# Two matrix products cut into quarter parts and spread between the steps of the RWKV-7 head loop

## The reference

```python
r, w, k, v, kk, a = ...              # 16 heads of 64, from the input projection
def frame_step(S, inp):              # RWKV-7, 256 steps
    sa = jnp.einsum('bhvk,bhk->bhv', S, -kk_t)
    S = S * w_t + sa[..., None] * (kk_t * a_t) + v_t[..., None] * k_t
    return S, jnp.einsum('bhvk,bhk->bhv', S, r_t)
o = group_norm(o) * ln_g + ln_b + bonus      # per head
o = o * g                                    # gate
y_rwkv = o @ w_rwkv_proj
y_conv = silu(layernorm(conv(...))) @ w_conv_proj
merged = gate0 * y_rwkv + gate1 * y_conv
x = x + merged @ w_out
```

## Time and profile before

| what | value |
|---|---|
| median of 3 runs | 1508.72 us |
| the profiled execution | 1513.77 us, of which the span 1512.0 us |
| PE busy | 1340.9 us (89%), 7904 matmuls |
| DVE, ACT, POOL busy | 856.9, 716.8, 606.2 us |
| mean granted PE clock | 0.942 |

### The profile page before, as it was taken

How to read it: one execution, slowest core, us unless ns; L and a number is a source line. 1 busy time by engine, 2 the same in 40 slices (tenths; PEclk the granted TensorE clock), 3 DMA queues, 4 the chain that set the end, 5 groups by cost and what they waited for, 6 DMA issues and landing times. The chain is left out here.

```text
span 1512.0 us, 22529 instructions
## 1 busy us (share of the span) xinstructions
PE 1340.9 (89%) x7904; PEld 1076.1 (71%) x7904; DVE 856.9 (57%) x1454; ACT 716.8 (47%) x1225; POOL 606.2 (40%) x324
## 2 busy tenths in 40 slices
PE   5989988788899999998759998867899988799996
PEld 4877877576677777776547775756788866678885
DVE  2292354434688888887341799995777753210112
ACT  4455455434477666766444333444333423344442
POOL 5859668540000000001357654734100006578784
PEclk9999998689899999999979998888999999899999
DMA  6637443037399999997356444542000005356562
GB/s 201 177 109 200 137 139 125 1 103 236 116 342 302 320 318 316 325 299 229 96 164 188 130 128 139 168 119 95 18 2 2 2 23 175 114 154 189 170 189 84
DMA packets 127271, 239.88 MB, mean 159 GB/s; under 512 B 16297, under 2 KB 32347, under 8 KB 127185
## 3 DMA queue, kind: packets, MB, share of 16 engines
q1 hardware_dynamic: 116384, 227.12, 48.0%
q10 hardware_dynamic: 10801, 11.60, 2.8%
HBM read 234.49 MB, written 1.05 MB: 156 GB/s over the span
## 5 line engine op out<-in xcount | busy, mean ns | idle before, releaser
L292 POOL TENSOR_TENSOR wlo<-raw,whi 128x1024 fp32r<-128x1024 f32 (+1 forms) x232 | 564.6, 2452 | 712.4 <-ACT whi L287 711.9
L298 PE MATMUL bank<-whi,t0h 128*128 128x512 f32 (+1 forms) x1072 | 440.2, 411 | 22.1 <-POOL wlo L292 6.2
L287 ACT ACTIVATE whi<-raw 128x1024 fp32r<-128x1024 f32 (+1 forms) x300 | 309.0, 1052 | 275.1 <-PE bank L300 231.2
L299 PE MATMUL bank<-wlo,t0h 128*128 128x512 f32 (+1 forms) x1072 | 429.0, 400 | 0.0
L300 PE MATMUL bank<-whi,t0l 128*128 128x512 f32 (+1 forms) x1072 | 428.8, 400 | 0.0
L298 PEld LDWEIGHTS bank<-whi,t0h 128*128 128x128 f32 x1072 | 206.7, 193 | 78.5 <-issue 23.7
L300 PEld LDWEIGHTS bank<-whi,t0l 128*128 128x128 f32 x1072 | 206.3, 192 | 48.6
L299 PEld LDWEIGHTS bank<-wlo,t0h 128*128 128x128 f32 x1072 | 206.5, 193 | 45.8 <-issue 1.7
L292 DVE TENSOR_TENSOR wlo<-work,whi 128x1024 fp32r<-128x1024 f32 x96 | 113.0, 1218 | 7.5 <-ACT whi L287 7.4
L287 ACT ACTIVATE whi<-work 128x1024 fp32r<-128x1024 f32 x96 | 97.9, 1055 | 5.1 <-PE bank L1460 5.1
L292 DVE TENSOR_TENSOR wlo<-raw,whi 128x1024 fp32r<-128x1024 f32 x68 | 80.2, 1219 | 13.8 <-ACT whi L287 13.8
(11 more groups left out here) (421 smaller groups left out, 1889.7 us busy)
## 6 DMA issues: line engine op xcount, KB each, us to landing
raw<-in_w_ff SPq DMA_DIRECT2D x64, 512.0 KB, 3.7
raw<-in_w_in SPq DMA_DIRECT2D x60, 496.0 KB, 3.6
raw<-in_w_in SPq DMA_DIRECT2D x56, 512.0 KB, 3.7
work<-in_w_exp_down SPq DMA_DIRECT2D x68, 256.0 KB, 6.2
work<-in_w_exp_gate SPq DMA_DIRECT2D x62, 256.0 KB, 5.9
work<-in_w_exp_up SPq DMA_DIRECT2D x62, 256.0 KB, 7.0
raw<-in_w_exp_down SPq DMA_DIRECT2D x60, 256.0 KB, 5.4
raw<-in_w_exp_gate SPq DMA_DIRECT2D x34, 256.0 KB, 6.0
```

Of the source, the lines that this page charges most:

```text
L287: nc.scalar.activation(whi[:, s, 0:width], raw_of(n)[:, 0:width], ACT.Copy).then_inc(hi_ready, 1)
L292: ins = (nc.vector if split_by_vector(n) else nc.gpsimd).tensor_tensor(wlo[:, s, 0:width], raw_of(n)[:, 0:width], whi[:, s, 0:width].bitca ...
L298: nc.tensor.matmul(dst, hi, wh, start=first, stop=False)
L299: nc.tensor.matmul(dst, hi, wl, start=False, stop=False)
```

## The change

The last two quarters of Q_CONV (6 and 7) leave `first()` and are multiplied in step 0, in eight parts of six matmuls' third each (`quarter_part`: one position tile and one row block, three matmuls), at the places where later steps have the tail. The second half of Q_CONV goes to banks 6 and 7, and its gating moves behind mask 4 of step 0. The grams of pair 0 come one quarter earlier, and their second pair uses banks 3 and 2 as in the other steps.

Q_RWKV is taken in another order (`RWKV_TILES`): quarters 0 to 3 are now both column halves of input rows 0 to 511, so all four need only the first four turned chunks. The first two are cut into parts and stand in pair 7's tail. Its splits move: quarters 2 and 3 are split on ACT inside step 0 (behind levels 3 and 5), and quarters 4 and 5 in pair 7's tail. The three rows move to slots 1 to 3, so that slot 0 takes quarter 4 early; DVE's wait for them moves behind step 0. The diff, cut to what bears on this:

```diff
@@ -313,6 +313,17 @@
...
+def quarter_part(pe, n, q, dst, hi, lo, part):
...
+    if part == 0:
+        wait_low(pe, n)
+    wh, wl = pair_view(whi, n, TW), pair_view(wlo, n, TW)
+    t, kk = part // 2, part % 2
+    k, r = 2 * q + kk, slice(t * P, (t + 1) * P)
+    mm = times(dst[t][:, 0:TW], hi[:, k, r], lo[:, k, r], wh[:, kk, :], wl[:, kk, :], k == 0, k == KC - 1)
+    if part == 3:
+        mm.then_inc(quarter_done, 1)
@@ -1811,13 +1822,26 @@
...
-    load_square(sp, Q_RWKV, A["w_rwkv_proj_2"][0], range(4))
-    for j, (dst, name) in enumerate(((ka_row, "k_a_2"), (lng, "ln_x_g_2"), (lnb, "ln_x_b_2"))):
+    w = A["w_rwkv_proj_2"][0].rearrange("(k p) n -> p k n", k=KC)
...
+    def rwkv(j):
+        q, c = RWKV_TILES[j]
+        load(sp, Q_RWKV + j, [(pair_view(raw, Q_RWKV + j, TW), w[:, 2 * q:2 * q + 2, c * TW:(c + 1) * TW])])
...
+    for j in range(4):
+        rwkv(j)
+    for j, dst, name in ((1, ka_row, "k_a_2"), (2, lng, "ln_x_g_2"), (3, lnb, "ln_x_b_2")):
...
+    rwkv(4)
+    sp.wait_ge(*tok_ready.at(2 * PAIRS))
+    rwkv(5)
...
-    load_square(sp, Q_RWKV, A["w_rwkv_proj_2"][0], range(4, 8))
+    rwkv(6)
+    rwkv(7)
...
+RWKV_TILES = ((0, 0), (0, 1), (1, 0), (1, 1), (2, 0), (3, 0), (2, 1), (3, 1))
@@ -2176,9 +2200,9 @@
...
-ka_row, lng, lnb = (raw[:, (Q_RWKV + j) % RING, :] for j in range(3))
+ka_row, lng, lnb = (raw[:, (Q_RWKV + j) % RING, :] for j in range(1, 4))
...
-ka_first = carve(10880, P)
+ka_first = carve(10880, 2 * P)
@@ -2207,7 +2231,7 @@
...
-    return bank[(3 if u > 1 and not (isinstance(p, int) and p == 0) else 5) - u % 2]
+    return bank[(3 if u > 1 else 5) - u % 2]
@@ -2253,7 +2277,7 @@
...
-            pe.wait_ge(*gram_masked.at(4 * p + 2))
+            pe.wait_ge(*evac2.at(NT * len(TILES2)))
@@ -2355,28 +2379,47 @@
...
         if tail:
+            if p == 1:
+                pe.wait_ge(*conv_gated.at(4))
             rest(p - 1, c, 0)
+        else:
+            pe.wait_ge(*conv_gated.at(2))
+            conv_part(6, 0)
         if prep:
...
             solve(p - 1, c, 0)
+        else:
+            conv_part(6, 1)
         below(p, b, 0, (1,))
...
             state(p - 1, c)
+        else:
+            conv_part(6, 2)
         below(p, b, 1)
...
             outputs(p - 1, c, 0, 0)
+        else:
+            conv_part(6, 3)
         grow(p, b, 1)
...
             outputs(p - 1, c, 0, 1)
+        else:
+            conv_part(7, 0)
         below(p, b, 2)
...
             rest(p - 1, c, 1)
+        else:
+            conv_part(7, 1)
         grow(p, b, 2)
...
             solve(p - 1, c, 1)
+        else:
+            conv_part(7, 2)
         below(p, b, 3)
+        if not tail:
+            conv_part(7, 3)
         if tail:
@@ -2399,18 +2442,32 @@
...
+    def conv_quarter(n):
+        if n < 4:
+            pe.wait_ge(*c_low.at(n + 1))
+        wide_quarter(pe, Q_CONV + n, n % 4, bank[0:2] if n < 4 else bank[6:8], t0h, t0l)
...
+    def conv_part(n, part):
+        quarter_part(pe, Q_CONV + n, n % 4, bank[6:8], t0h, t0l, part)
...
+    def rwkv_part(j, part):
+        q, c = RWKV_TILES[j]
+        quarter_part(pe, Q_RWKV + j, q, bank[2 * c:2 * c + 2], t0h, t0l, part)
...
-        prepare = {0: lambda: decays(0), 2: lambda: turn_ar(0), 3: lambda: turn_bk(0, 0),
-                   5: lambda: grams(0, 0, (0, 1)), 6: lambda: grams(0, 0, (2, 3))}
-        for n in range(8):
-            if n < 4:
-                pe.wait_ge(*c_low.at(n + 1))
-            wide_quarter(pe, Q_CONV + n, n % 4, bank[2 * (n // 4):2 * (n // 4) + 2], t0h, t0l)
-            if n in prepare:
-                prepare[n]()
-        pe.wait_ge(*conv_gated.at(4))
+        conv_quarter(0)
+        decays(0)
+        conv_quarter(1)
+        conv_quarter(2)
+        turn_ar(0)
+        conv_quarter(3)
+        turn_bk(0, 0)
+        conv_quarter(4)
+        grams(0, 0, (0, 1))
+        conv_quarter(5)
+        grams(0, 0, (2, 3))
@@ -2433,20 +2490,28 @@
...
+        pe.wait_ge(*y_masked.at(2 * LEV * PAIRS))
+        pe.wait_ge(xt_copied, XT_COPIES * PAIRS)
+        pe.wait_ge(*turn_h.done(2))
+        rwkv_part(0, 0)
...
+        rwkv_part(0, 1)
+        rwkv_part(0, 2)
...
+        rwkv_part(0, 3)
+        rwkv_part(1, 0)
...
-        pe.wait_ge(*y_masked.at(2 * LEV * PAIRS))
-        pe.wait_ge(xt_copied, XT_COPIES * PAIRS)
-        for n in range(8):
-            if n < 4:
-                if n == 2:
-                    turn_h.pe(pe, [heads_gated.at(4), pair_done.at(PAIRS), (uo_copied, 2 * PAIRS)], (2, 3))
-                pe.wait_ge(*turn_h.done(2 * n + 2))
-            wide_quarter(pe, Q_RWKV + n, n % 4, bank[2 * (n // 4):2 * (n // 4) + 2], t0h, t0l)
+        for part in range(1, 4):
+            rwkv_part(1, part)
+        for j in range(2, 8):
+            if j == 4:
+                turn_h.pe(pe, [heads_gated.at(4), pair_done.at(PAIRS), (uo_copied, 2 * PAIRS)], (2, 3))
+            if j in (4, 5):
+                pe.wait_ge(*turn_h.done(2 * j - 2))
+            for part in range(4):
+                rwkv_part(j, part)
@@ -2518,12 +2583,16 @@
...
             head_roots(0)
+        if not tail:
+            split_high(act, Q_RWKV + 2)
         if prep:
...
         grown(p, b, 5)
+        if not tail:
+            split_high(act, Q_RWKV + 3)
         diagonal(p, b)
@@ -2537,7 +2606,7 @@
...
-        for q in range(4):
+        for q in range(2):
@@ -2555,7 +2624,9 @@
...
         copy_u(p, 1)
+        split_high(act, Q_RWKV + 4)
         head_roots(1)
+        split_high(act, Q_RWKV + 5)
@@ -2701,6 +2772,8 @@
...
+        else:
+            gate_convolution(1)
@@ -2741,7 +2814,7 @@
...
-            nc.vector.tensor_tensor(o, o, bank[2 * c + t][:, :], ALU.mult).then_inc(conv_gated.sem, 1)
+            nc.vector.tensor_tensor(o, o, bank[6 * c + t][:, :], ALU.mult).then_inc(conv_gated.sem, 1)
@@ -2758,9 +2831,8 @@
...
-        gate_convolution(1)
+        step(0, 0, tail=False)
...
-        step(0, 0, tail=False)
@@ -2926,7 +2998,7 @@
...
-        dve.wait_ge(quarter_done, Q_RWKV + 4 * c + 4)
+        dve.wait_ge(quarter_done, Q_RWKV + 2 * c + 6)
```

More of the change, by code:

```diff
@@ L1990, in act_in2 @@
                                  bias=taps2[:, 248 + K2 - 1:248 + K2]).then_inc(chunk_done, 1)
-            act.dma_start(ka_first, row(A["k_a_2"][0, 0:P], P)).then_inc(rk_loaded, 16)
+            act.dma_start(ka_first, row(A["k_a_2"][0, 0:2 * P], 2 * P)).then_inc(rk_loaded, 16)
         def shift(dve, order, p):
@@ L2226, in decays @@
             def decays(p):
-                if not (isinstance(p, int) and p == 0):
-                    pe.wait_ge(*gram_masked.at(4 * p - (2 if p > 1 else 0)))
+                if p:
+                    pe.wait_ge(*gram_masked.at(4 * p - 2))
                 for t in range(NT):
@@ L2597, in key_direction @@
             def key_direction(p):
-                ka = row_of(ka_first if isinstance(p, int) and p == 0 else ka_row, p)
+                ka = row_of(ka_first if isinstance(p, int) and p < 2 else ka_row, p)
                 order.mark(nc.vector.scalar_tensor_tensor(out=tmpb, in0=gain_a[:, :, ds(P * p, P)], scalar=-1.0,
@@ L2881, in act_out2 @@
             turn_h.act(act, Q_RWKV, range(4, 8))
-            for q in range(4, 8):
+            for q in range(6, 8):
                 split_high(act, Q_RWKV + q)
```

## The result

The changed kernel takes 1518.15 us (median of 13 runs), the kernel before 1510.57 us on the same chip (13 runs). The ratio is 1.0043, with a 95% interval of 1.0028 to 1.0058: slower, by 0.43% or some 6.5 us (4.2 to 8.8 by the interval; the two medians alone are 7.6 us apart). On the 1508.72 us that the forecast of 1507.5 started from, that is 1515.2. The profiled execution has a span of 1518.2 us (1520.04 in all) and a mean granted clock of 0.934, against 1512.0 and 0.942.

The account below looks back on a forecast made before the run. PE was taken as full in steps with a tail, while step 0's chain waits for DVE and ACT. Terms -5.4 + 2.9 - 0.5 + 1.8 = -1.2 on 1508.72 gave 1507.5 us, own range 1505 to 1510.

Parts of the forecast that it names:

- The term for the clock (+1.8): PE after the new waits: one stretch at half clock in all, +1.8 us, with bounds of 0 and +7.
- step 0's term (-5.4): Projection's end and step 0: PE's wait shrinks and the parts mostly hide in the chain's waits, -5.4 us.
- the parts don't hide: Rival for step 0: its links don't overlap the parts, sum +0.6 us, 1509.3 us; chance 0.10.
- The rows, +2.9: Step 1: DVE waits for the late `lnb` row ahead of its first mask and PE stands, +2.9 us, bounds 0 and +4.0.
- Pair 7's tail, -0.5: Pair 7's tail to the merge: +1.2 us up to the last quarter, -1.7 at the merge, together -0.5 us.
- The merge: Behind the last quarters, up to its turn: meets POOL's splits once, not twice, 4.6 us where 6.25 before, -1.7 us.
- slower by the clock: Rival: half speed follows each of the three waits, 8.5 us in place of 1.8, sum +5.5, 1514.2 us; chance 0.17.
- own signs of being wrong: No wait in step 1, last gating under 3 us later, or granted clock below 0.9 in both steps 0 and 1.

Follow-up runs that it names:

- e8_whole: The changed kernel with e1_row_wait's edit, and convolution quarters 6 and 7 multiplied whole ahead of step 0's first `below`: ratio 0.9959 to the kernel before.
- e1_row_wait: The changed kernel, but DVE waits behind step 0 for the k_a row alone, the two other rows being awaited where read: ratio 1.0002 to the kernel before.
- e2_fill: The changed kernel with its row wait kept and ten unread 512-column matmuls put into PE's gap in step 1: ratio 1.0008 to the kernel before.
- e3: The changed kernel with pair 7's tail, the Q_RWKV order and the splits of quarters 4 and 5 as before: ratio 1.0035 to the kernel before.
- e5: The changed kernel with the edits of e1_row_wait and e3 together, leaving only the parts in step 0: ratio 0.9996 to the kernel before.
- e9: The changed kernel with e8_whole's edits and the old tail of e3: ratio 0.9936 to the kernel before.
- e6_late_splits: The changed kernel with e1_row_wait's edit, and Q_RWKV quarters 4 and 5 split only behind DVE's last gatings: ratio 0.9970 to the kernel before.
- e7_tiles: The changed kernel with e1_row_wait's edit, whole Q_RWKV quarters behind pair 7's outputs, the turn behind the third, early splits: ratio 1.0019 to the kernel before.
- e4: The changed kernel with all eight convolution quarters ahead of step 0 as before, its new tail kept: ratio 1.0010 to the kernel before.

## Why the prediction was wrong

Two steps of it failed. The term for the clock (+1.8) was too small, because its premise, that no row shows a short wait followed by half clock, was false, and the changed kernel had three stretches of half clock, worth 8.3 us. And step 0's term (-5.4) counted on room for the parts that the chain didn't have.

**Step 0, -5.4 (failed).** The start came out as worked out: the wait is 2.16 us (2.3 predicted), and the inverse begins while one split of POOL is met instead of two. What failed is the sentence that its chain "waits for DVE and ACT and leaves PE room". The earlier trace rows had shown PE busy for 16.51 of 16.91 us, and I read the clock of 0.90 as a sign of room; the busy time of slowed matmuls is no room either way, and e8_whole shows 0.7 us of it at full clock. Six parts at 0.90 are 5.4 us and, by an estimate from these rows, all but about 1 us of it lay on the path: 14.9 us of bare chain behind the second `below` (15.2 less 0.3), 5.4 of parts and some 1.4 for a stretch at half clock (1058.76 to 1062.01 took 3.25 us for two `below` and a part, that are 1.9 elsewhere) make 21.7, and 20.55 were measured. The clock's share of that is counted below; the parts' own miss is 1.3 us (-5.4 to -2.7, less 1.4). The rival "the parts don't hide" had step 1's first row at 1078.8; it came at 1079.31, or 1079.74 counted from before's D0, with the 1.4 us of clock in it.

**The rows, +2.9 (right as an idle time, wrong as a cost).** Every link of the chain came as predicted; the load landed 4.1 us after its issue instead of 3.6, and PE was due a little later, since it had already waited 0.36 us. e1_row_wait shows the wait to be the cause, and e2_fill what it costs without the clock: 2.3 us (23.01 less 20.71, with DVE's wait half a microsecond shorter). The 0.4 us beside POOL's split had no term.

**Pair 7's tail, -0.5 (its work right, its clock not).** The turn was forecast 6.86 us later in its stretch than before (1252.35 against 1245.49) and came 7.15 later: 35.41 us from V7 against 28.26. Part of that agreement is luck: the outputs came 3.4 us later where 2.7 was forecast, and DVE's chain behind them grew by 3.7 where 4.2 was forecast, and PE waited 2.69 us, not 3.7. The splits fell across DVE's chain on the instructions named, L2792 and L2801. The merge takes 4.56 us where 4.6 was forecast; it takes 4.65 or 4.66 in e3, e5 and e9 too, whose tail is that of before, so this gain does not come from the tail's parts. Between the two stands the miss: from the turn to the last quarter's end 13.45 us were forecast (1252.35 to 1265.8), and 15.81 were measured at a granted clock of 0.79. At 1.00 the same piece takes 14.07 us in e6_late_splits, whose PE doesn't wait ahead of the turn; PE is busy for 12.67 us of it against 15.07, 2.4 less (by length only 1.7, since PE waits more there). That is 2.4 of the 2.6 us between -0.5 and +2.1. The other traces bear out that the wait brought it on, rather than chance. PE waits 2.67 to 2.75 us ahead of the turn in five executions and 5.05 in e7_tiles, and in each the clock from the turn to the last quarter is under 1.00 (after 0.79, e1 0.79, e2 0.89, e4 0.80, e8 0.79, e7 0.83). In the other seven PE waits at most 1.05 us there, and the clock is 1.00. Ahead of the turn the clock varies without any such change: tails of the same code differ by 2.2 us (52.67 and 54.87).

**The clock, +1.8 (the step that decides, mis-sized).** The sum allowed one stretch of half clock in all, since "that a wait under 3 us does it, no row shows (1.05 and 1.16 did not)". That was misread. The third window of the earlier trace rows, whose 6.8 us at half clock the prediction puts down to "a long wait", holds no wait above 1.81 us. The timeline of before, PE, and its windows there:

```profile
1223.36 0.45 PE L2299 MATMUL bank<-work 64*64 64x64 f32 x8 [1.81 <-DVE work L2656]
...
1226.33 1.11 PE L2309 MATMUL bank<-work 64*64 64x64 f32 x8 [1.07 <-DVE work L2654]
...
1225.00:1226.00 1.00, 0.26 (x4) 0.12 (x2) 0.97 (x3) 0.71 (x2) 0.00 (x0) 1.00 0.00 0
1226.00:1227.00 1.00, 0.67 (x6) 0.67 (x7) 0.48 (x2) 0.00 (x0) 0.00 (x0) 0.53 0.00 0
...
1233.00:1234.00 1.00, 1.00 (x11) 1.00 (x11) 1.00 (x4) 0.00 (x0) 0.00 (x0) 1.00 0.00 0
```

Elsewhere in the same trace a wait of 2.22 us (to 405.33) was followed by half clock too, while one of 2.83 us (to 337.02) was not. So waits of this size could have been priced, as likely and not as certain.

In the changed kernel there were three stretches of half clock, one behind each of the three waits: 1.4 us in step 0 (a wait of 2.16 us, followed by 0.50 in all seven traces that have it), 4.5 in step 1, 2.4 behind the turn (15.81 less 13.45). That is 8.3, and the rival "slower by the clock" had 8.5. Put into the sum in place of 1.8, with 1.3 us more for the parts that step 0 did not hide and 0.4 for the wait beside POOL's split, -1.2 becomes +7.0, and the stretches show +6.9. So two rivals came true together. That their totals fit is partly luck: the rival had its long stretches at 3.4 us each, and step 1's was 4.5 here and 6.0 in e3_tail_undone. The prediction's own signs of being wrong did not catch this either: step 1 had its wait, the last gating came late, and the granted clock fell below 0.9 in step 1 (0.82) but not in step 0 (0.93).

The Trainium skill (SBUF — State Buffer, Who interferes with whom) says that of a DVE instruction with two SBUF inputs and a GpSimd instruction that reads SBUF the one that starts first holds the shared pair, and the other "fully blocks". The rows agree: L2801 becomes ready at 1251.04 while a split has run since 1250.49, and ends 1.08 us after that split, a little under its own length of 1.23. L2792, which has one input only, ended with the split beside it as well.

## What to carry to other kernels

Before work is moved into a chain "with room", subtract PE's busy time at full clock from the stretch: a stretch with a granted clock under 1.00 looks longer than it is, and its room is only what is left when the clock is back. A new wait in front of full PE can cost its length and then the clock (here 2.6 us of idle time cost 7.1): before its price is set, list every wait of its size in the trace at hand with the granted clock behind it, and give it the clock's stretch, or put matmuls into it. A wait on one semaphore for several loads should be cut so that each reader waits only for its own, and POOL's splits should stand behind the DVE chain that an engine is waiting for. A split that waits for PE should not stand ahead of ACT's share of that chain.

## What the runs showed that I had not expected

- PE idle for 2.61 us (and 2.42 in e3_tail_undone), with small matmuls round it, was followed by a granted clock of 0.82 (0.77) over the step; ten 512-column matmuls in the same gap kept it at 1.00, and the step was 4.8 us shorter. The Trainium skill (TensorE: Matmul & The Clock Gate, What's actually happening) says of the ramp at a kernel's start that for modeling it is under 1% of a typical span, and not to fit a count of slow matmuls. No run here looks at the start; the one stretch in step 1 is 4.5 us, 0.3% of this span, and also most of what decided this change.
- Three 512-column matmuls put alone between 64-column ones take 0.90 us, where they take 0.70 in a row of their own kind: 0.34 us behind the first and 0.32 behind the last instead of 0.235.
- A DVE instruction on 128x16 elements took 1.80 us instead of 0.17 beside a POOL split.
- The clock can fall without a wait: in e4_tail_alone it was 0.50 for close to 7 us at the start of step 7, where PE had no wait above 0.34 us, and D3 to V7 took 3.0 us longer.
